# A recurrent state chain with two state buffers, half-width products and its norms moved, in a fused two-block kernel

## The reference, cut to what matters

```python
def rwkv7_step(state, inp):
    r_t, w_t, k_t, v_t, kk_t, a_t = inp
    sk = jnp.einsum('bhij,bhj->bhi', state, kk_t)
    state = (state * w_t[:, :, None, :]
             - sk[..., None] * (kk_t * a_t)[:, :, None, :]
             + v_t[..., None] * k_t[:, :, None, :])
    y = jnp.einsum('bhij,bhj->bhi', state, r_t)
    return state, y
...
    o = rms_norm(o, g_attn_out.reshape(MLA_HEADS, MLA_V))
...
    mu = jnp.mean(y, axis=-1, keepdims=True)
    var = jnp.mean(jnp.square(y - mu), axis=-1, keepdims=True)
    y = (y - mu) * lax.rsqrt(var + LN_X_EPS) * ln_x_w + ln_x_b
    y = (y + bonus) * g
    x = x + jnp.concatenate([y_a, y_b], axis=-1) @ w_o[l]
```

## Time and profile before

| what | value |
|---|---|
| median of 3 runs | 2992.51 us (2990.03 to 2999.43) |
| profiled execution | 2994.27 us, span 2992.3 us |
| PE busy | 2514.9 us, 84% |
| DVE busy | 1542.2 us, 52% |
| ACT busy | 705.3 us, 24% |
| mean granted clock of PE | 0.955 |

### The profile page before, as it was taken

The page is one execution under the profiler, slowest core; times in us unless marked ns, Lnnn a source line. Parts: engine busy times, 40 slices in busy tenths (PEclk is TensorE's granted clock), DMA queues, the critical chain, the costliest instruction groups (busy, mean ns, idle before and its releaser), DMA issues. The chain is left out here.

```text
span 2992.3 us, 24901 instructions
## 1 busy us (share of the span) xinstructions
PE 2514.9 (84%) x8676; PEld 1169.8 (39%) x8676; DVE 1542.2 (52%) x3247; ACT 705.3 (24%) x2014; POOL 527.3 (18%) x516
## 2 busy tenths in 40 slices
PE   6799389699997777777777777777799888999998
PEld 3355289544542222222222222222244333444443
DVE  3644774621266665676667675544419366333204
ACT  1022221100113333433333334433300101111000
POOL 0000000000014344444444344333200000000000
PEclk9899698699989999999999999999999998999999
DMA  3200000032299999999999999999811211221220
GB/s 123 98 8 29 28 3 2 29 119 98 87 348 422 421 421 421 421 421 421 420 416 420 416 414 418 422 419 419 346 56 57 105 56 57 84 85 62 79 71 28
DMA packets 126830, 656.24 MB, mean 219 GB/s; under 512 B 9456, under 2 KB 12144, under 8 KB 60912
## 3 DMA queue, kind: packets, MB, share of 16 engines
q0 software_dynamic: 73728, 536.90, 43.3%
q1 hardware_dynamic: 52976, 117.74, 11.1%
HBM read 652.51 MB, written 2.10 MB: 219 GB/s over the span
## 5 line engine op out<-in xcount | busy, mean ns | idle before, releaser
L712 PE MATMUL PD<-AR,C 128*128 128x512 f32 x2048 | 1008.6, 619 | 277.1 <-ACT C L997 276.0
L1560 DVE CUSTOM_DVE_ANT_0 AR<-AR,HN 128x1024 f32<-128x1024 f32 x512 | 626.1, 1223 | 486.7 <-DMA AR<-in_uv,C 484.0
L1700 POOL DMA_INDIRECT AR<-in_uv,C x512 | 527.1, 1030 | 1622.2 <-DVE C L1478 860.6
L712 PEld LDWEIGHTS PD<-AR,C 128*128 128x128 f32 x2048 | 351.6, 190 | 931.3 <-ACT C L997 662.4
L444 PE MATMUL PA<-HT,WR 128*128 128x512 f32 x736 | 327.8, 605 | 3.0 <-ACT HT L817 2.1
L444 PE MATMUL PA<-AR,WR 128*128 128x512 f32 (+1 forms) x720 | 314.7, 605 | 6.4 <-ACT AR L888 4.9
L991 ACT ACTIVATE SC<-SC 128x1 f32<-128x1 f32 x512 | 103.9, 203 | 763.3 <-DVE SC L1560 762.9
L444 PEld LDWEIGHTS PA<-HT,WR 128*128 128x128 f32 x736 | 141.9, 194 | 179.6 <-issue 177.1
L444 PEld LDWEIGHTS PA<-AR,WR 128*128 128x128 f32 (+1 forms) x720 | 138.8, 194 | 181.8 <-issue 179.0
L997 ACT ACTIVATE C<-C,SC 128x128 f32<-128x128 f32 x512 | 205.5, 401 | 16.7
L993 ACT ACTIVATE SC<-SC,C 128x1 f32<-128x1 f32 x512 | 150.8, 295 | 16.6
(11 more groups left out here) (325 smaller groups left out, 2051.7 us busy)
## 6 DMA issues: line engine op xcount, KB each, us to landing
WR<-in_w_ada SPq DMA_DIRECT2D x12, 2048.0 KB, 8.1
WR<-in_w_in SPq DMA_DIRECT2D x11, 2048.0 KB, 7.9
WR<-in_w_up SPq DMA_DIRECT2D x11, 2048.0 KB, 7.8
WR<-in_w_down SPq DMA_DIRECT2D x5, 2048.0 KB, 7.8
WR<-in_w_pq SPq DMA_DIRECT2D x4, 2048.0 KB, 7.9
AR<-in_uv,C POOLq DMA_INDIRECT x512, 15.3
WR<-in_w_o SPq DMA_DIRECT2D x2, 2048.0 KB, 7.7
WR<-in_w_out SPq DMA_DIRECT2D x2, 2048.0 KB, 7.7
```

What stands on the lines that cost most here:

```text
L712: ins = nc.tensor.matmul(acc[half], DG[:, j, :], UV[:, j, D + 512 * half:D + 512 * half + 512], start=(k == 0), stop=(k == NSEL - 1))
L1560: ttr(UV[:, j, 0:D], UV[:, j, 0:D], HN[:, t, :], 1.0, 0.0, ALU.mult, ALU.add, DOT[:, j:j + 1]).then_inc(s["dots"], 1)
L1700: nc.gpsimd.indirect_dma_start(UV[:, turn % RING, :], None, uv, bass.IndirectOffsetOnAxis(ap=IDX[:, t % 2, i:i + 1], axis=0),).then_inc(uv ...
```

## The change

- The state has two buffers, `tmid` and a free part of HN, used in turn. DVE multiplies the old state by the decay into the new buffer before the state product is there, then adds the product block by block, eight 64x64 operations. The identity product, the mask and the wait for this chunk's output product go; PE waits on a new semaphore `state`. The last chunk makes no state.
- The products of the chain are issued in halves: 64 weight columns for output partitions 0 to 63 and 64 for 64 to 127. The state product makes only the two diagonal blocks. The matrices of a chunk alternate between the array's row halves.
- The attention norm runs on DVE between the operations of inversion levels 1 to 4: squares and sums of two tiles and their variance in level 1, the same for the other two in level 2, roots and scalings in levels 3 and 4. ACT's roots go behind its copies of levels 2 and 3.
- All four output norms come behind the state updates on DVE, and ACT's roots for three of them behind all chain copies, ahead of the SiLU.

```diff
--- before.py
+++ after.py
@@ -73,7 +73,7 @@
     ("hT", 4, 4), ("pm", 4, 4), ("cT", 3, 2), ("q", 4, 4), ("kv", 4, 4), ("qkT", 12, 8),
     ("att", 40, 64), ("pr", 2, 0), ("lora", 12, 0), ("kn", 0, 4), ("bonus", 0, 1),
     ("tok", 4, 8),
-    ("inv", 32, 48), ("chain", 12, 28),
+    ("inv", 32, 48), ("chain", 12, 27),
     ("yT", 8, 4), ("wo", 4, 12), ("pq", 8, 8), ("s", 16, 0), ("ada", 8, 0),
     ("modc", 0, 1), ("acc", 8, 8), ("in2", 24, 4), ("ln", 0, 2), ("pw", 0, 8),
     ("yb", 0, 8), ("wout", 4, 12), ("up", 44, 0), ("down", 4, 4), ("end", 0, 0),
...
@@ -320,6 +320,7 @@
         DOT = small(RING)
         GEL = small(RING)
         csil2 = small(8)
+        STATE = [tmid, HN[:, NT - 1, 512:1024]]
         ffst = small(14 * NT)
 
 
@@ -609,47 +610,59 @@
 
                 sl = slice(P * c, P * c + P)
                 for left, right in ((KT, KK), (KT, RT), (AT, RT)):
-                    for odd in range(2):
-                        b = bank("d")
-                        o = 64 * odd
-                        for q in range(4):
-                            ins = nc.tensor.matmul(b[:, P * q:P * q + P], left[o:o + 64, q, sl],
+                    both = [bank("d"), bank("d")]
+                    for q in range(4):
+                        for odd in range(2):
+                            o = 64 * odd
+                            ins = nc.tensor.matmul(both[odd][:, P * q:P * q + P], left[o:o + 64, q, sl],
                                                    right[o:o + 64, q, sl], start=True, stop=True)
-                        full("d", ins)
+                            if q == 3:
+                                full("d", ins)
+
+            def in_halves(b, hv, pairs):
+
+                for i, (lhsT, rhs) in enumerate(pairs):
+                    for o in (0, 64):
+                        ins = nc.tensor.matmul(b[o:o + 64, hv], lhsT[:, o:o + 64], rhs, start=(i == 0),
+                                               stop=(i == len(pairs) - 1))
+                return ins
 
             matrices(0)
             pe.wait_ge(s["d_free"], fd)
-            pe.wait_ge(s["tmid"], 2)
+            pe.wait_ge(s["tmid"], 3)
             for c in range(NT):
                 sl = slice(P * c, P * c + P)
                 mat, f_, sk_ = MATS[c % 2], FS[c % 2][:, 0, :], FS[c % 2][:, 1, :]
+                st_ = STATE[c % 2]
                 heads = [(h, slice(64 * h, 64 * h + 64)) for h in range(H)]
                 pe.wait_ge(s["d_free"], fd + 7 * c + 6)
+                if c > 0:
+                    pe.wait_ge(s["state"], 8 * c)
                 b = bank("a")
                 for h, hv in heads:
-                    nc.tensor.matmul(b[:, hv], KK[:, h // 2, sl], tmid[:, hv], start=True, stop=False)
-                    ins = nc.tensor.matmul(b[:, hv], mat[:, 0, h, :], VTOK[:, c, hv], start=False, stop=True)
+                    ins = in_halves(b, hv, [(KK[:, h // 2, sl], st_[:, hv]), (mat[:, 0, h, :], VTOK[:, c, hv])])
                 full("a", ins)
                 if c + 1 < NT:
                     matrices(c + 1)
                 pe.wait_ge(s["a_free"], fa + 3 * c + 1)
                 b = bank("a")
                 for h, hv in heads:
-                    ins = nc.tensor.matmul(b[:, hv], XT(h)[:, sl], f_[:, hv], start=True, stop=True)
+                    ins = in_halves(b, hv, [(XT(h)[:, sl], f_[:, hv])])
                 full("a", ins)
                 pe.wait_ge(s["a_free"], fa + 3 * c + 2)
-                b = bank("d")
-                for pr in range(4):
-                    f2 = slice(P * pr, P * pr + P)
-                    nc.tensor.matmul(b[:, f2], ident, tmid[:, f2], start=True, stop=False)
-                    nc.tensor.matmul(b[:, f2], KTOK[:, c, f2], VTOK[:, c, f2], start=False, stop=False)
-                    ins = nc.tensor.matmul(b[:, f2], BTOK[:, c, f2], sk_[:, f2], start=False, stop=True)
-                full("d", ins)
+                if c + 1 < NT:
+                    b = bank("d")
+                    for pr in range(4):
+                        for i, (lhsT, rhs) in enumerate(((KTOK[:, c, :], VTOK[:, c, :]), (BTOK[:, c, :], sk_))):
+                            for o in (0, 64):
+                                hv = slice(P * pr + o, P * pr + o + 64)
+                                ins = nc.tensor.matmul(b[o:o + 64, 64 * pr:64 * pr + 64], lhsT[:, hv], rhs[:, hv],
+                                                       start=(i == 0), stop=(i == 1))
+                    full("d", ins)
                 b = bank("a")
                 for h, hv in heads:
-                    nc.tensor.matmul(b[:, hv], RT[:, h // 2, sl], tmid[:, hv], start=True, stop=False)
-                    nc.tensor.matmul(b[:, hv], mat[:, 1, h, :], VTOK[:, c, hv], start=False, stop=False)
-                    ins = nc.tensor.matmul(b[:, hv], mat[:, 2, h, :], sk_[:, hv], start=False, stop=True)
+                    ins = in_halves(b, hv, [(RT[:, h // 2, sl], st_[:, hv]), (mat[:, 1, h, :], VTOK[:, c, hv]),
+                                            (mat[:, 2, h, :], sk_[:, hv])])
                 full("a", ins)
 
             def modulation(w):
@@ -919,13 +932,14 @@
                     if lev > 1:
                         act.wait_ge(s["d_full"], FIRST_D["inv"] + 4 + 8 * (lev - 2) + 2 * q + 2)
                     tell(nc.scalar.copy(ZI[rows, q, :], b[rows, :]), "a_free")
+                if lev in (2, 3):
+                    roots(cosb[:, 32 * (lev - 2):32 * (lev - 2) + 16])
 
             for c in range(NT):
                 for dst in (FS[c % 2][:, 0, :], FS[c % 2][:, 1, :], HN[:, c, 512:1024]):
                     tell(nc.scalar.copy(dst, take()), "a_free")
+            for c in range(NT - 1):
                 roots(st_a[:, 16:24])
-                if c > 0:
-                    roots(st_a[:, 16:24])
 
             tell(A(csil2, vv("c"), ACT.Silu), "act")
             link()
@@ -1290,6 +1304,51 @@
                 tell(nc.vector.tensor_copy(BTOK[:, t, :], take()), "d_free")
             fa, fd = FIRST_A["inv"], FIRST_D["inv"]
 
+            def heads_of(z):
+                return z.rearrange("p (h d) -> p h d", h=H)
+
+            def attention_squares(t):
+
+                o3 = heads_of(HN[:, t, 0:512])
+                link(tt(heads_of(tmid), o3, o3, ALU.mult))
+                at = 32 * (t // 2) + 8 * (t % 2)
+                link(nc.vector.tensor_reduce(cosb[:, at:at + 8], heads_of(tmid), AX, ALU.add))
+
+            def attention_variance(p):
+
+                v_ = cosb[:, 32 * p:32 * p + 16]
+                link(ts(sinb[:, 32 * p:32 * p + 16], v_, 1.0 / 64, EPS, ALU.mult, ALU.add))
+                tell(nc.vector.tensor_copy(v_, sinb[:, 32 * p:32 * p + 16]), "var")
+
+            def attention_rstd(p, roots_done):
+
+                v_, w_, r_ = cosb[:, 32 * p:32 * p + 16], sinb[:, 32 * p:32 * p + 16], sinb[:, 32 * p + 16:32 * p + 32]
+                dve.wait_ge(s["rstd"], roots_done)
+                link(nc.vector.reciprocal(r_, v_))
+                link(tt(w_, w_, r_, ALU.mult))
+                link(stt(w_, w_, -0.5, r_, ALU.mult, ALU.mult))
+                link(stt(v_, w_, 1.5, r_, ALU.add, ALU.mult))
+
+            def attention_scale(t):
+
+                o3 = heads_of(HN[:, t, 0:512])
+                at = 32 * (t // 2) + 8 * (t % 2)
+                link(tt(o3, o3, cosb[:, at:at + 8].unsqueeze(2).broadcast_to([P, H, 64]), ALU.mult))
+                link(tt(HN[:, t, 0:512], HN[:, t, 0:512], r1("g_attn"), ALU.mult))
+
+            def attention_norm(lev, q):
+
+                if lev < 3:
+                    if q < 2:
+                        attention_squares(2 * (lev - 1) + q)
+                    elif q == 2:
+                        attention_variance(lev - 1)
+                elif lev < 5:
+                    if q == 0:
+                        attention_rstd(lev - 3, n["var"] - (4 - lev))
+                    elif q < 3:
+                        attention_scale(2 * (lev - 3) + q - 1)
+
             def blocks(z):
                 return z.rearrange("p (c n) -> p c n", c=8)
 
@@ -1300,7 +1359,6 @@
             dve.wait_ge(s["rhat"], 4)
             dve.wait_ge(s["a_free"], FIRST_A["lora"] + 12)
             tell(nc.vector.memset(XTS[64:128, :, :, 0:64], 0.0), "tmid")
-            tell(nc.vector.memset(tmid[:, :], 0.0), "tmid")
             for q in range(4):
                 b = take()
                 link(tt(blocks(XI[:, q, :]), blocks(b), mask64(LOW0), ALU.mult), "d_free")
@@ -1330,26 +1388,19 @@
                         tell(tt(XI[:, q, :], XI[:, q, :], b, ALU.add), "d_free")
                         dve.wait_ge(s["a_full"], fa + 8 + 4 * (lev - 1) + q + 1)
                         tell(tt(blocks(CTL[:, q, :]), blocks(MT[:, q, :]), mask64(LV[:, lev + 1, :]), ALU.mult), "ct")
+                        attention_norm(lev, q)
             for q in range(4):
                 b = take()
                 tell(nc.vector.tensor_copy(XTS[0:64, q, :, 64:128], blocks(b[0:64, :])), "d_free")
 
```

(48 more changed lines are left out.)

## The result

The changed kernel takes **2952.4 us** (median of 4 runs, 2951.1 to 2954.1) where the kernel before, on the same chip, takes 2991.3 us: a ratio of 0.9865, with a 95% interval of 0.9846 to 0.9884. The forecast was 2952 us, in a range of 2942 to 2981. The profiled execution has a span of 2950.0 us against 2992.3, that is 42.3 us less.

A forecast was written before the change was run, and what follows sets the result against it. PE was taken to bound the kernel, busy 84% of the span, its clock below full in the chain. +9.0 - 0.3 - 58.7 + 9.5 = -40.5 us gave 2953.7 profiled, 2952 us on the median's scale, range 2942 to 2981.

The forecast's parts named there:

- Half products: Chain products on PE: alternating halves of 64 weight columns run side by side at 0.029 us a pass, 864 passes.
- Rivals one and three: Chain passes: halves one after the other, 0.058 us, 2977 us (chance 0.15); half costs a whole, 0.112, 3024 (0.05).
- rival one: Chain products: halves run one after the other, 0.058 us a pass, 2977 us in all; chance 0.15.
- Clock: PE in the chain: dense halves keep the granted clock at 1.00 over most of it.
- rival two: Chain: halves overlap but the clock stays at 0.50, 0.058 us a pass, 2980 us in all; chance 0.12.
- Chain: State chain on PE: ends at 515.7 instead of 574.45, -58.7 us, allowing 2 us for gaps and 2.5 for low clock.
- State updates: DVE in each chunk: eight 64x64 updates at 0.2 us each, 1.6 us, covered by the output product.
- 0.3 us each: State updates on DVE: if each took 0.3 us, 0.1 us a chunk would come back.
- Inversion: Levels 1 to 4: attention norm between DVE's trios makes levels 14.0 and 14.4 us instead of 11.91, +9.0 us.
- Memset: The removed memset gives back 0.3 us of its 0.49.
- Behind the chain: PE waits 22.8 us for the SiLU, which ACT makes after three output norms' roots, against 13.3 before: +9.5 us.
- Rival four: Chain: passes cost what they do today, only 15 us of waits go against 18.2 of other costs: 2995 us; chance 0.04.

The follow-up runs named there:

- experiment 2: The changed kernel with the chain's half products reordered, lower output halves of all heads first, then the upper: 2973.4 us.
- Experiment 1: The changed kernel with whole products of 128 weight columns in the chain instead of halves, all else kept: 2982.6 us.
- experiment 5: The changed kernel with the attention norm behind each level's last mask, and SiLU broadcast and first output norm's root ahead of ACT's last chain copy: 2920.6 us.
- experiment 7: The changed kernel with one wait put back: DVE updates the state only after the chunk's output product: 2961.2 us.
- experiment 3: The changed kernel with the attention norm's operations of a level all behind the fourth group's mask instead of between the groups: 2941.8 us.
- experiment 4: The changed kernel with the SiLU made after level 1 copies, its broadcasts and the first output norm's root before ACT's last chain copy: 2929.7 us.

## Why the prediction was right, step by step

- **Half products.** Taken at 0.029 us a pass from the alternating quarters of the inversion, measured 0.030. Rivals one and three (0.058, 0.112) are out, and experiment 2 shows that rival one is what the other order gives. The Trainium skill's page "TensorEngine Tiling (Array Packing)", section Tiling Modes, which lets different tiles load and multiply in parallel, is what the trace agrees with. The rule of the Trainium skill's page "TensorE: Matmul & The Clock Gate", Part 3, that a weight load overlaps a matmul in flight only where the row group differs, fails here: the two halves share all their rows, and a pass takes 0.030 us where they alternate against 0.054 where they don't.
- **Clock.** Expected 1.00 over most of the chain, measured 1.00 in all four chunks; rival two is out. The reason given, dense halves, is not shown. Experiment 1 has 1.00 in its middle chunks with whole products. Alternating halves did meet a low clock, at the chain's start in experiment 5 and behind one pause of three in experiment 7, and so did the quarter products of level 4 in the change. What the runs show is less: behind the same pause of 2.75 us the clock fell three times of three with whole products and once with halves. Why it falls in one place and not in a like one stays open, and that it was 1.00 in the change's whole chain may be luck in part.
- **Chain.** Without allowances the formula gave 40.8 us from first product to last copy; it took 42.0. Of the 4.5 us added for small gaps and a low clock 1.2 were used. The chunks were put at 11.0 and 7.6 us and took 11.45 and 7.67, from first product to first product and to the last copy. The mask group with its change of tile shape took 3.7 us, at 3.5; the copies 0.91, at 0.9.
- **State updates.** Mis-sized: 1.6 us for eight, measured 2.49, 0.31 each. The nearest row's overlap (0.2 us each) doesn't hold for operations that read PSUM at this size. It cost next to nothing, as the branch "0.3 us each" said: they end at 494.06, 0.1 us before the next chunk's first product, which starts some 0.1 us late.
- **Inversion.** +9.0 expected, and 0.5 for the masks of chunk 0. From DVE's first operation of level 1 to that of level 5 it was +10.0 (47.3 to 57.3 us), from there to the chain's first product +0.8. Levels 1 and 2 took 13.69 us each, at 14.0; levels 3 and 4 took 14.32 and 15.59, at 14.4 each. What no step had foreseen is the last one's clock, 0.50 in one stretch of level 4:

```profile
460.80:464.20 3.40, 3.40 (x57) 3.40 (x54) 0.35 (x1) 0.43 (x1) 0.00 (x0) 0.50 0.00 0
```

The mean over level 4 (448.26 to 463.85) is 0.90. That the norm's *place* and not its amount makes the cost is shown by experiment 3, where the same work costs nothing; the prediction had named the place ("stands between the trios").
- **Memset.** 0.3 us were to come back; the stretch up to level 1 shows +2.0, with 1 DVE operation less. That offset begins before any code that the change touches, and -2.6 us come in the last stretch, equally untouched; neither is put down to the change. They nearly cancel.
- **Behind the chain.** +9.5 expected, 22.8 us of idle PE; measured 22.64, +9.3. The roots stand 8.94 us apart as read from the earlier trace rows. The step of ACT's order is shown by experiment 4.
- **Rival four**, that only 15 us of waits would go, is out on both counts. Its sum had two flaws. The third chunk's 7.7 us compare a window without its wait of 1.3 us with one that has it; from copy to copy the third is 6.5 us longer than the second (26.15 and 32.68). And the 48 passes that the change drops, 5.4 us at full clock, stand in no term of it. Without half products 31.8 us went: these passes, the waits, and the low clock in two chunks.
- **The total.** 40.5 us were expected and 42.3 measured, closer than the terms are. The inversion with the first masks was put at +9.5 and cost 10.8; the chain from first product to last copy was put at -59.2 (45.3 us) and gave -62.5. These misses point opposite ways, so part of the closeness is luck. The terms listed for the forecast's own range add up to 2945.5 to 2960, not 2943 to 2963; nothing hangs on it.

## What to carry to other kernels

A float32 product with few moving columns (here 64 for 128 weight columns) is bound by its weight load (0.112 us a pass with 64 moving columns, 0.111 with 128); split into two halves of 64 weight columns which alternate in the queue, it takes 0.060 us for the pair of passes instead of 0.112, and nearly all of it is the order: 0.108 with the halves one after the other. What moves into a stage with slack has to go where the slack is, behind the last operation that the next product waits for, and an engine's small operation that another engine waits for must be looked up in its program's order: both changes of order here were worth 1.2% together, on top of a change worth 1.35%. A pause of PE is priced with the clock behind it: 2.75 us cost 3.3 us on average between dense halves (2.8, 2.8 and 4.4) and 7.1 us between whole products.

## What was not expected of the hardware

- With the norm behind the trios a level takes 11.20 us, which is 12 groups of 0.93 without any gap, less than the 11.91 us of the kernel before, in which DVE had less to do. PE's small gaps of that kernel (11.71 us busy in a level of 11.91, with groups broken up by single passes) are not there. Why more work on DVE removes them stays open.
- Two column halves that share all their rows overlap, 0.030 us a pass against 0.054 when neighbours write the same half.
- The granted clock fell behind the same pause of 2.75 us in every chunk of whole products and behind one of three with halves (0.89 in that chunk). It also fell with no wait above 0.68 us in front of it, in the last chunk of experiment 1 (0.50 over 12.4 us).
